# Attention scores of two units made together, in two halves of each PSUM bank

## What is computed

```python
def window_attention(qg, kk, vv, bias, valid, sinks):
    s = einsum('...qkgd,...skd->...kgqs', qg, kk) * HEAD_DIM ** -0.5 + bias
    s = where(valid, s, -inf)
    m = maximum(max(s, axis=-1), sink)
    e = exp(s - m[..., None])
    p = e / (sum(e, axis=-1) + exp(sink - m))[..., None]
    return einsum('...kgqs,...skd->...qkgd', p, vv)

kv = rmsnorm(x, kv_norm) @ w_kv
q = rmsnorm(x, norm_mix[l]) @ w_q[j]
o = window_attention(...)
x = x + o @ w_attn_out[j]
```

## Time and profile before

| what | value |
|---|---|
| median of 3 runs | 2265.55 us (2264.87 to 2266.0) |
| profiled execution, its own time | 2264.82 us |
| its span | 2263.0 us |
| TensorE (PE) busy | 98% of the span, weight loads (PEld) 94% |
| DVE busy | 66% |
| ACT busy | 48% |
| POOL busy | 14% |
| mean DMA rate | 115 GB/s |
| the attention loop, first scores to last values | 1269.2 to 1531.8 us |

### The profile page before, as it was taken

One profiled execution on the slowest core, in us unless ns is written; L12 is line 12 of the kernel. 1 busy time (PEld: TensorE's weight loads), 2 busy tenths in 40 slices (PEclk: granted clock), 3 DMA queues, 4 the chain that ended last, 5 costly groups with the idle time before them and its releaser, 6 DMA issues. The chain is left out here.

```text
span 2263.0 us, 41252 instructions
## 1 busy us (share of the span) xinstructions
PE 2212.0 (98%) x16742; PEld 2122.8 (94%) x16742; DVE 1504.3 (66%) x2546; ACT 1081.2 (48%) x2130; POOL 305.9 (14%) x333
## 2 busy tenths in 40 slices
PE   7999999999999999999999999989999999999998
PEld 7999998888999999999999877869999999999998
DVE  6555555679755567778956676475856566788873
ACT  5233332336666664434433454254666665343435
POOL 1000000013322220000001011013122221000003
PEclk9999999999999999999999999999999999999999
DMA  4222121212232327756722311101233335675651
GB/s 125 67 71 71 59 72 42 68 39 68 94 114 96 114 95 283 245 181 215 234 76 67 86 38 45 38 10 47 81 109 105 104 115 207 231 242 197 195 181 78
DMA packets 221520, 260.63 MB, mean 115 GB/s; under 512 B 27759, under 2 KB 144412, under 8 KB 220788
## 3 DMA queue, kind: packets, MB, share of 16 engines
q1 hardware_dynamic: 220596, 253.61, 34.8%
q10 hardware_dynamic: 736, 4.38, 0.6%
HBM read 216.16 MB, written 46.97 MB: 116 GB/s over the span
## 5 line engine op out<-in xcount | busy, mean ns | idle before, releaser
L2793 PE MATMUL acc<-t_hi,w_lo 128*128 128x264 f32 x1568 | 447.0, 285 | 0.0
L2792 PE MATMUL acc<-t_lo,w_hi 128*128 128x264 f32 x1568 | 446.8, 285 | 0.0
L2791 PE MATMUL acc<-t_hi,w_hi 128*128 128x264 f32 x1568 | 444.7, 284 | 0.0
L2791 PEld LDWEIGHTS acc<-t_hi,w_hi 128*128 128x128 f32 x1568 | 295.9, 189 | 0.0
L2793 PEld LDWEIGHTS acc<-t_hi,w_lo 128*128 128x128 f32 x1568 | 294.6, 188 | 0.0
L2792 PEld LDWEIGHTS acc<-t_lo,w_hi 128*128 128x128 f32 x1568 | 294.5, 188 | 0.0
L2757 PE MATMUL acc<-x_lo,w_hi 128*128 128x264 f32 x896 | 254.6, 284 | 0.0
L2758 PE MATMUL acc<-x_hi,w_lo 128*128 128x264 f32 x896 | 254.5, 284 | 0.0
L2756 PE MATMUL acc<-x_hi,w_hi 128*128 128x264 f32 x896 | 254.4, 284 | 0.0
L2512 PE MATMUL acc<-x_hi,w_hi 128*128 128x352 f32 x576 | 191.9, 333 | 1.4 <-DVE pair L1979 1.4
L2756 PE MATMUL acc<-T_hi,w_hi 128*128 128x264 f32 x672 | 190.9, 284 | 0.2
(11 more groups left out here) (393 smaller groups left out, 5509.1 us busy)
## 6 DMA issues: line engine op xcount, KB each, us to landing
w_raw<-in_w_down SPq DMA_DIRECT2D x72, 512.0 KB, 5.1
w_raw_odd<-in_w_down SPq DMA_DIRECT2D x70, 512.0 KB, 4.9
b<-h_rows SPq DMA_DIRECT2D x42, 528.0 KB, 6.4
w_third<-in_w_down SPq DMA_DIRECT2D x34, 512.0 KB, 4.4
h_rows<-z_even SPq DMA_DIRECT2D x32, 528.0 KB, 2.7
w_raw<-in_w_up SPq DMA_DIRECT2D x32, 512.0 KB, 4.3
w_raw_odd<-in_w_up SPq DMA_DIRECT2D x32, 512.0 KB, 5.1
w_raw<-in_w_mlstm_in SPq DMA_DIRECT2D x24, 512.0 KB
```

Source lines behind the costliest of these rows:

```text
L2791: T.matmul(out[:, h], hi[:, c, rows], mh[:, c, v], start=(g == 0 and c == 0), stop=False)
L2792: T.matmul(out[:, h], hi[:, c, rows], ml[:, c, v], start=False, stop=False)
L2793: x = T.matmul(out[:, h], lo[:, c, rows], mh[:, c, v], start=False, stop=(g == KG - 1 and c == 1))
```

## The change

The odd unit's scores get the other half of the same two banks (columns 256 to 511), so that two units' scores can stand in banks 4 and 5 at once. TensorE makes the scores of units u + 1 and u + 2 together in each odd iteration u, and none in even ones (before the loop: units 0 and 1). `s_ready` is raised by 2 after the pair, and only the even unit of a pair waits for `mx_ready`. DVE reads the even unit at the place in the odd iteration where it stood, and the odd unit in the same iteration behind the DVE part of the dense window; in even iterations it has no maxima.

```diff
@@ DVE, maxima @@
-                    x = V.tensor_tensor_reduce(prob[:, r, e, lo:2 * WIN], acc[:, 4 + e, lo:2 * WIN], bias[:, 4 * e + n % 4, lo:],
+                    at = 2 * WIN * (u % 2)
+                    x = V.tensor_tensor_reduce(prob[:, r, e, lo:2 * WIN], acc[:, 4 + e, at + lo:at + 2 * WIN], bias[:, 4 * e + n % 4, lo:],
@@ DVE, the loop @@
             maxima(0)
+            maxima(1)
             for u in range(UNITS + 3):
                 if 1 <= u <= UNITS:
                     probabilities(u - 1)
                 if u >= 3:
                     outputs(u - 3)
-                if u + 1 < UNITS:
+                if u % 2 == 1 and u + 1 < UNITS:
                     maxima(u + 1)
                 att_dense(att_window(u))
+                if u % 2 == 1 and u + 2 < UNITS:
+                    maxima(u + 2)
                 for gp in range(2):
                     sample(gp, u - SAMPLE_AT[gp])
@@ TensorE, scores @@
-                if u > 0:
+                if u > 0 and u % 2 == 0:
                     pe.wait_ge(mx_ready, u)
                 for e in range(2):
                     h = slice(HD * e, HD * e + HD)
-                    x = T.matmul(acc[:, 4 + e, lo:256], q_t[h, n % 2, cols(b)],
+                    at = 2 * WIN * (u % 2)
+                    x = T.matmul(acc[:, 4 + e, at + lo:at + 2 * WIN], q_t[h, n % 2, cols(b)],
                                  k_t[h, gp, P * b - P + lo:P * b + P], start=True, stop=True)
-                x.then_inc(s_ready, 1)
+                if u % 2 == 1:
+                    x.then_inc(s_ready, 2)
@@ TensorE, the loop @@
             scores(0)
+            scores(1)
             for u in range(UNITS + 3):
-                if u + 1 < UNITS:
+                if u % 2 == 1 and u + 1 < UNITS:
                     scores(u + 1)
+                    scores(u + 2)
                 att_dense(att_window(u))
```

## The result

The changed kernel takes 2269.71 us (median of 11 runs, 2267.79 to 2274.62), the kernel before beside it 2266.0 us (11 runs, 2263.98 to 2267.53). The ratio is 1.0022, 95% interval 1.0015 to 1.0030. That is slower, by 3.7 us going by the medians and by 5.0 us going by the ratio, where no change was forecast. The time itself lies in the forecast range (2262.5 to 2270.8).

A forecast was written before the change was run, and what follows sets the result against it. TensorE, its matmuls filling 98% of the span, was taken as the bound. Joins saving 5.2 us against +6.1 of other terms, mostly waits on DVE, gave +0.9: 2265.7 profiled, 2266.4 for the median, range 2262.5 to 2270.8.

The forecast's parts named there:

- The saving of a join: TensorE's joined scores: the second unit needs no entry and takes 0.43 us, not 0.63, so each join saves 0.20.
- This rival (0.08): Joined scores: second unit's weight loads wait for the first's passes, so the join saves nothing; 2271.7 us, chance 0.08.
- 0.20 us to spare in a plain pair: Plain pairs with dense chunks: the new wait on DVE's moved maxima is hidden, with 0.20 us to spare.
- The rival "not there" (0.13): Semaphore seen 0.3 us later, so some 11 plain pairs wait too: +2 to +3 us, 2268.5; chance 0.13.
- Evictions: Iterations 5, 13, 21: eviction plus moved maxima on DVE make TensorE wait 0.49 us each, 1.5 in all.
- Sample steps 2 and 6: Iterations 25 and 29: odd maxima, 0.82 us, go ahead of the copy TensorE waits for; 1.6 in all.
- Iteration 35: Maxima ahead of probabilities move transposes of unit 35 from +6.48 to +7.30 us after the scores' start: 0.8.
- Iteration 53: Transposes of unit 53: DVE's chain starts 0.43 us later and is 0.82 longer, costing 1.25.
- The stretch without dense chunks: Where DVE and TensorE take turns: the dense chunk of 1527.25 comes 0.2 us later, bounds 2 us either way.
- The start: Scores(1)'s wait of 1.07 us for maxima(0) goes, but transposes(1) then wait about 0.8: net -0.3.
- Longer waits cost clock: Rival: longer TensorE waits in iterations 36 and 54 lower the granted clock, 1.6 us a fall; 2269.7 to 2271.3, chance 0.14.
- Waits that don't come: Rival: early odd maxima let ACT and DVE run ahead, so evictions and samples don't delay probabilities; 2260.3 us, chance 0.07.

The follow-up runs named there:

- the mixed version: The change, but with the odd unit's maxima at their old place in iterations where a TensorE wait on DVE follows: 2259.96 us, ratio 0.9973 to the kernel before.

## Why the prediction was wrong

Point by point:

- **What bounds the kernel** was right: every microsecond of TensorE counted, in both directions.
- **The saving of a join**, 0.20 us with 0.43 for the second unit: measured 1.06 for the two. All eight loads of a pair lie within 0.73 us, and the second unit adds the 0.43 that the prediction gave it. The rule of the Trainium skill's page "TensorE: Matmul & The Clock Gate", Part 3, which spoke against the join, is not what this trace shows. This rival (0.08) is out.
- **0.20 us to spare in a plain pair**: right; no transposes wait there, and the mixed version shows the place to be free. The rival "not there" (0.13) is out.
- **Evictions** 0.49 each: measured 0.45 and 0.46. **Sample steps 2 and 6**, 0.82 each: from 0.71 to 1.52 and from 1.25 to 2.06, 0.81 each. **Iteration 35**, +7.30: 1397.77 is 7.28 behind the joined scores at 1390.49. **Iteration 53**, 6.88: 6.91 behind 1495.13. **The stretch without dense chunks**, +0.2: with the waits filled, from transposes(53) at 1500.30 to the dense chunk at 1527.80 is 27.50, before 1527.25 - 1500.12 = 27.13, so +0.4 (with bounds of 2 us). **The start**: the gap of 1.07 is gone, and the transposes of unit 1 wait 0.65 where about 0.8 was worked out.
- **The sum**, +0.9: +0.5 in the attention loop, and 2266.62 against 2266.05 for the whole kernel, once the change's additional falls are gone by filling.
- **The step that failed** is the clock. The sum gave it no term, so it put the cost of the longer waits in clock at nothing, and left it to a rival ("Longer waits cost clock", 0.14, which "decides from the second additional fall on"). The mechanism stood in that rival, with its place and its price of 1.6 us a fall, and both medians lie in its 2269.7 to 2271.3 us. The only reason given against it was one case, the wait of 1.45 us in iteration 36 that cost no clock, though the forecast waits, 2.2 and 1.9, were longer than that one. The sign that the prediction named for being wrong, a granted clock under 1.00 in more stretches than the one at 1372, is the one that came. Measured: 5.2 us more clock lost per execution than before, and 4.2 us go when the waits are filled, against a loss of 3.7 to 4.8.
- **Waits that don't come** (0.07): out.
- **Where luck came in.** That the time lies in the forecast range is no merit of the sum: the range took in a second fall of the clock, while the account behind the forecast had none.

What stays open: which of the waits brings a fall in a given execution. In the loops of the ten profiled executions 15 waits of 1.88 to 2.33 us were left unfilled, and 9 of them were followed by a fall. Behind the loop, between long groups of matmuls, every one of the ten has a wait of 2.2 us (1583 us in the changed kernel), and only 2 show a fall there. Falls also come far from the changed code: the profiled execution of the change has one from 476 to 484 us, that of the kernel before has none there, but one at 1228.

## What to carry to other kernels

A sum of busy times and waits that comes out near zero is not yet a forecast of no change: list each wait of TensorE that gets longer, and give the loss of clock behind it a term of its own (here as likely as not for a wait of about 2 us among short groups of matmuls). A change can be two changes: here the join gained 5.5 us alone, and the place of one read on DVE took back 10.3, almost twice that; try them apart. Work moved ahead of what a waiting engine needs next costs about its full length there (here 0.81 of 0.82 us at the sample steps), even where it is free elsewhere.

## What the runs showed of the hardware

- Matmuls into the same two row groups and the same two banks, in other columns, run on without a pause that the profile shows: two units' scores, with eight weight loads, took 1.06 us, against 0.63 for one.
- TensorE waits of 1.25 to 2.33 us, each between short groups of matmuls, were followed by stretches at 1.2 GHz in some executions and not in others: 9 of 15 times for those of 1.88 us and more. The same kernel on the same chip lost between 13.6 us of clock (0.994) and 20 us (0.991) per execution, and its time ran from 2268.2 to 2274.7 us with it, 0.3% for one binary.
- What a fall of the clock costs in time differs by place: 1.6 us of clock lost near 1372, among waits, were 1.0 us of time, and 1.7 us lost near 1399, with dense chunks behind the wait, were 1.55 us.
- 66 matmuls of no use, placed in waits that stayed, made the kernel 4.2 us faster.
